# One pass for both norms between the blocks, all taps of three tiles on VectorE, and a layer norm that goes last tile first

## What is computed

```
x = x + gate * attention_output                     # end of block 1
x = rmsnorm(x, final_norm_g)                        # norm A
h = rmsnorm(x, norm_mix_g_2[0])                     # norm B, of the result of norm A
p = h @ w_in_ab_2                                   # a: 512 columns, v: 512, gate: 512
ya = fnet(a)                                        # two DFTs, then a 128x128 map per head
u = v * sigmoid(gate)                               # 4 tiles of 128 channels x 256 tokens
u = depthwise_conv(u, 31 taps) + conv_b
u = layernorm(u over the 128 channels of its tile)  # then silu
x = x + concat(ya, silu(u)) @ w_out_ab_2            # then the first FFN
```

## Time and profile before

| | us |
|---|---|
| median of 3 runs (753.13 to 753.42) | 753.21 |
| the profiled execution, its own time | 753.22 |
| its span, first to last instruction | 751.3 |
| PE busy in it | 724.5 (96%) |
| DVE busy | 509.6 (68%) |
| ACT busy | 396.2 (53%) |

### The profile page before, as it was taken

How to read it: one execution, slowest core, us unless ns; L and a number is a source line. 1 busy time by engine, 2 the same in 40 slices (tenths; PEclk the granted TensorE clock), 3 DMA queues, 4 the chain that set the end, 5 groups by cost and what they waited for, 6 DMA issues and landing times.

```text
span 751.3 us, 9715 instructions
## 1 busy us (share of the span) xinstructions
PE 724.5 (96%) x3898; PEld 626.4 (83%) x3898; DVE 509.6 (68%) x794; ACT 396.2 (53%) x622; POOL 2.4 (0%) x8
## 2 busy tenths in 40 slices
PE   2999999999899999999999999999999999999996
PEld 2888889999899999878888888888788888888885
DVE  5889997998876989986744545454576544545444
ACT  4157446864875677755644344433665344344423
POOL 0000000000000000000000000000000000000000
PEclk9999999999999999999999999999999999999999
DMA  8999983899643525213755445544226455455201
GB/s 339 425 427 413 425 361 147 305 388 348 273 134 149 205 91 210 84 36 161 280 174 203 182 171 198 191 167 172 109 112 224 168 183 205 172 173 198 77 0 57
DMA packets 23229, 156.65 MB, mean 208 GB/s; under 512 B 2576, under 2 KB 2832, under 8 KB 5264
## 3 DMA queue, kind: packets, MB, share of 16 engines
q1 hardware_dynamic: 22608, 153.41, 54.1%
q0 software_dynamic: 576, 2.62, 1.0%
HBM read 154.97 MB, written 1.05 MB: 208 GB/s over the span
## 4 chain that ended last, share of the span: by engine, by line
PE 80%; DVE 10%; ACT 6%; issue 2%; DMA 2%; SPq 0%; DVEq 0%; ACTq 0%
PE pb L1562 20%; PE pb L1563 19%; PE pb L1564 19%; PE pb L1636 13%; DVE w L1009 4%; PE pb L1832 2%; ACT w L611 2%; PE pb L1933 1%; DVE raw L1012 1%; DMA raw<-w_dram 1%; DMA x<-x_dram 1%; DVE t L1009 1%; DVE x L1012 1%; PE pb L1863 1%; PE pb L1875 0%
## 5 line engine op out<-in xcount | busy, mean ns | idle before, releaser
L1009 DVE TENSOR_TENSOR w<-raw,w 128x2048 fp32r<-128x2048 f32 x97 | 221.2, 2290 | 143.6 <-ACT w L611 143.6
L611 ACT ACTIVATE w<-raw 128x2048 fp32r<-128x2048 f32 x97 | 184.8, 1912 | 143.3 <-PE pb L1564 119.2
L1562 PE MATMUL pb<-w,r 128*128 128x512 f32 (+1 forms) x640 | 246.5, 385 | 0.7 <-DVE r L1012 0.4
L1563 PE MATMUL pb<-w,r 128*128 128x512 f32 (+1 forms) x640 | 243.3, 380 | 0.0
L1564 PE MATMUL pb<-w,r 128*128 128x512 f32 (+1 forms) x640 | 243.2, 380 | 0.0
L1562 PEld LDWEIGHTS pb<-w,r 128*128 128x128 f32 x640 | 120.5, 188 | 25.6 <-issue 1.8
L1564 PEld LDWEIGHTS pb<-w,r 128*128 128x128 f32 x640 | 120.5, 188 | 24.7
L1563 PEld LDWEIGHTS pb<-w,r 128*128 128x128 f32 x640 | 120.6, 188 | 23.3
L1562 PE MATMUL pb<-r,w 128*128 128x256 f32 (+1 forms) x352 | 100.3, 285 | 1.0 <-DVE r L1009 0.5
L1563 PE MATMUL pb<-r,w 128*128 128x256 f32 (+1 forms) x352 | 99.4, 282 | 0.0
L1564 PE MATMUL pb<-r,w 128*128 128x256 f32 (+1 forms) x352 | 99.0, 281 | 0.0
(11 more groups left out here) (191 smaller groups left out, 582.6 us busy)
## 6 DMA issues: line engine op xcount, KB each, us to landing
raw<-w_dram SPq DMA_DIRECT2D x129, 1024.0 KB, 4.9
ow<-w_dram SPq DMA_DIRECT2D x8, 1024.0 KB, 15.2
ow<-w_dram SPq DMA_DIRECT2D x8, 512.0 KB, 16.7
oh<-w_dram SPq DMA_DIRECT2D x2, 1024.0 KB, 22.6
x<-x_dram SPq DMA_DIRECT2D x2, 512.0 KB, 5.7
f<-rc_dram POOLq DMA_DIRECT2D x1, 1024.0 KB, 5.0
acc<-row_dram POOLq DMA_DIRECT2D x2, 512.0 KB, 5.2
out_dram<-f SPq DMA_DIRECT2D x4, 256.0 KB, 2.3
```

The costliest lines, as they stand in the source:

```text
L611: return e.activation(out, in_, ACT.Copy, **kw)
L1009: return e.tensor_tensor(out, a, b, op)
L1562: e.matmul(out, a_hi, b_hi, start=start, stop=False)
L1563: e.matmul(out, a_hi, b_lo, start=False, stop=False)
```

## The change

1. Both norms from one pass. `two_squares` makes X² and (g X)² on ACT, `two_adds` sums both on DVE during `project`; PE sums them over channels with four one-column matmuls (`two_sums`), so norm A and norm B are both columns of 128x2. ACT and DVE take roots and reciprocals on those columns, and PE spreads the two results to rows with four 128x128 matmuls (`two_rows`). The second round of squares and adds, and the two reciprocals of 128x256, are gone. Slabs 22 and 23 are done one after the other (`single`), not as a pair.
2. DVE does all 31 taps of tile 2; PE's 12 diagonal taps of it and their addition are gone.
3. The layer norm takes the variance as columns (two one-column matmuls a tile), root and reciprocal on 128x2, and PE spreads the result (`ln_row`, two 128x128 matmuls a tile). The order is tile 3 first, alone, then 0, 1, 2 in groups. `mixed` takes kt 7 before kt 4, and ends with kt 5 and 6.
4. The key projection keeps its raw hi half in a buffer of its own (`KR`) with the shift column beside it; the lo half of the shift is a second column of it. `R2` has no spare columns left. ACT, not DVE, copies the first half of the output into X.

```diff
-NPE = 12
-LN = (0, 1, 3, 2)
+LN = (3, 0, 1, 2)
...
+            def two_squares(d):
+                for m in range(2):
+                    n = 2 * (d - 1) + m
+                    if n >= NT:
+                        p.wait_ge(s_na, 7 + n - NT + 1)
+                    to = tt[n % NT] if d else NA[m]
+                    kw = {"scale": V("final_norm_g", d)} if m else {}
+                    e.activation(to[:, :], X[:, d, :], ACT.Square, **kw).then_inc(s_sq, 1)
...
-                copy(kb[:, d:d + 1], bank_of("k", d)[:, T:T + 1]).then_inc(s_kb, 1)
+                copy(k2[:, :], bank_of("k", d)[:, T:T + 2], accum_out=kb[:, d:d + 1]).then_inc(s_kb, 1)
...
-            row_close(2)
-            col_close(0, rcol[:, 0:2])
+            p.wait_ge(s_rtc, 1)
+            e.reciprocal(rcol[:, 0:2], rcol[:, 0:2]).then_inc(s_rcl, 1)
+            p.wait_ge(s_rcl, 1)
+            tt_(rcol[:, 2:4], sums[:, 2:4], rcol[:, 0:2], MUL).then_inc(s_col, 1)
+            p.wait_ge(s_col, 1)
+            tt_(rcol[:, 2:4], rcol[:, 2:4], rcol[:, 0:2], MUL).then_inc(s_col, 1)
...
+            p.wait_ge(s_rtc, 2)
+            e.reciprocal(rcol[:, 2:4], rcol[:, 2:4]).then_inc(s_rcl, 1)
+            p.wait_ge(s_rcl, 2)
+            tt_(rcol[:, 4:6], rcol[:, 0:2], rcol[:, 2:4], MUL).then_inc(s_col, 1)
             fill(20)
-            p.wait_ge(s_rs, 3)
+            p.wait_ge(s_rsb, 1)
...
             for d in range(2):
                 gated(d, F1[:, 6 + d, :], F1[:, 4 + d, :], (s_b, d + 1), (s_b, d + 3))
+            fill(21)
             for d in range(2, 4):
                 gated(d, out_of("b", 2 + d), out_of("b", 4 + d), ended("b", 2 + d), ended("b", 4 + d))
             fill(22)
...
-            head(20, run("b", 0, 1, 2, 3), 0, lambda: close(2, 0))
-            head(22, run("b", 4, 5, 6, 7), 0, lambda: close(3, 1))
+            first = run("b", 0, 1, 2, 3)
+            pair(20, first, R2, s_rlo, 0, range(6), last=False)
+            two_sums()
+            pair(20, first, R2, s_rlo, 0, range(6, 8), first=False)
+            two_rows()
+            single(22, run("b", 4, 5), R2, s_rlo, 0)
+            single(23, run("b", 6, 7), R2, s_rlo, 0)
...
             def ln_var(d):
                 p.wait_ge(s_lnq, LN.index(d) + 1)
-                e.matmul(PB[OUT.bank["ln", d]][:, 256:512], ones, tt[d][:, :], start=True,
-                         stop=True).then_inc(s_lnv, 1)
+                for a in range(2):
+                    done = e.matmul(bank_of("ln", d)[:, T + a:T + a + 1], tt[d][:, a * P:a * P + P], ones_sb[:, 0:1],
+                                    start=True, stop=True)
+                done.then_inc(s_lnv, 1)
+
+            def ln_row(d):
+                p.wait_ge(s_lni, LN.index(d) + 1)
+                for a in range(2):
+                    done = spread(bank_of("ln", d)[:, T + a * P:T + a * P + P], lnr[:, d, a:a + 1])
+                done.then_inc(s_lnb, 1)
...
+            both(0)
             ln_var(3)
+            both(1)
+            ln_row(3)
+            both(2)
+            ln_mean(0, (s_tap, tap_at[0, 30]))
+            ln_mean(1, (s_tap, tap_at[1, 30]))
             mixed(3, 0, 0, 1)
+            ln_mean(2, (s_tap, tap_at[2, 30]))
             mixed(3, 1, 0, 1)
+            for d in range(3):
+                ln_var(d)
+            mixed(7, 0, 0, 1)
+            for d in range(3):
+                ln_row(d)
+            mixed(7, 1, 0, 1)
+            both(4)
             for a in range(2):
                 for c in range(2):
                     if a and c:
                         turn(0, 0)
-                    for kt in range(4, 8):
+                    for kt in (5, 6):
                         mixed(kt, c, a)
```

More of the change, by code:

```diff
@@ L359, in two_block_program @@
         root = sb("root", [P, T])
-        RS = [sb(f"rs{i}", [P, T]) for i in range(2)]
+        RSt = sb("rs", [P, 2, T])
+        RS = [RSt[:, i, :] for i in range(2)]
         NA = [sb(f"na{i}", [P, T]) for i in range(2)]
@@ L709, in _ @@
             p.wait_ge(s_mv, 11)
[L710 to L712 removed]
+            copy(raw_shift[:, :, 0], mv[:, 4, :]).then_inc(s_shh, 1)
             for d in range(8):
                 p.wait_ge(s_x1, d + 1)
[L715 to L716 removed]
+                e.activation(raw_key(d)[:, 0:T], X[:, d, :], ACT.Copy, scale=mv[:, 3, d:d + 1]).then_inc(s_khi, 1)
+                square(d)
             stream(MATS[2])
@@ L1198, in _, with project @@
                     y_tile(d)
-            def project(kind, i, done, scale, before, raw_, streams):
+            def project(kind, done, scale, before, raw_, add_, streams):
                 for d in range(8):
@@ L1403, in _ @@
             fill(22)
-            pump(12)
-            for c in range(2):
-                fill(24 + c)
-                pump(10)
-            for h in range(4):
-                pump(3)
-            pump(62 - tap_n["n"])
+            pump(36)
+            fill(24)
+            pump(20)
             for h in range(4):
@@ L1787, in _, with two_sums, two_rows @@
             block_of("ao", 16, R1, s_olo, paired=True)
-            def head(k, names, base, then):
-                pair(k, names, R2, s_rlo, base, range(4), last=False)
-                then()
-                pair(k, names, R2, s_rlo, base, range(4, 8), first=False)
-            def close(i, c):
-                row_sum(i)
-                col_sums(c, i)
-            head(20, run("b", 0, 1, 2, 3), 0, lambda: close(2, 0))
-            head(22, run("b", 4, 5, 6, 7), 0, lambda: close(3, 1))
+            def two_sums():
+                bank_free("ns", 0)
+                p.wait_ge(s_na, 7 + 14)
+                for m in range(2):
+                    for a in range(2):
+                        done = e.matmul(bank_of("ns", 0)[:, 2 * m + a:2 * m + a + 1], NA[m][:, a * P:a * P + P],
+                                        ones_sb[:, 0:1], start=True, stop=True)
+                done.then_inc(s_ps, 1)
+            def two_rows():
+                bank_free("rb", 0)
+                p.wait_ge(s_col, 3)
+                for i, c in ((0, 0), (1, 4)):
+                    for a in range(2):
+                        o = i * T + a * P
+                        done = spread(bank_of("rb", 0)[:, o:o + P], rcol[:, c + a:c + a + 1])
+                done.then_inc(s_ps, 1)
+            first = run("b", 0, 1, 2, 3)
[5 more added lines that the diff above has]
+            single(23, run("b", 6, 7), R2, s_rlo, 0)
             for c in range(2):
@@ L1891, in mixed, with both @@
                     done.then_inc(s_half, 1)
-            ln_mean(2, (s_cv2, 1))
-            mixed(0, 0, 0, 1)
-            mixed(0, 1, 0, 1)
-            mixed(1, 0, 0, 1)
+            def both(kt):
+                for c in range(2):
+                    mixed(kt, c, 0, 1)
+            both(0)
             ln_var(3)
-            ln_var(2)
-            mixed(1, 1, 0, 1)
-            mixed(2, 0, 0, 1)
-            mixed(2, 1, 0, 1)
+            both(1)
[3 more added lines that the diff above has]
+            ln_mean(1, (s_tap, tap_at[1, 30]))
             mixed(3, 0, 0, 1)
+            ln_mean(2, (s_tap, tap_at[2, 30]))
             mixed(3, 1, 0, 1)
+            for d in range(3):
+                ln_var(d)
+            mixed(7, 0, 0, 1)
+            for d in range(3):
+                ln_row(d)
+            mixed(7, 1, 0, 1)
+            both(4)
             for a in range(2):
```

339 lines of the change are left out of this document (160 added, 179 removed).

## The result

The changed kernel takes 741.1 us in the median of 4 runs (740.83 to 742.27), the kernel before 753.32 beside it (753.13 to 753.83): ratio 0.984, 95% interval 0.9823 to 0.9857. That is 12.2 us, not 4.8, and outside the predicted range.

What follows compares the result with a forecast made beforehand. The prediction took PE to bound the seam; its terms summed to -5.14 us, +0.3 charged for tight places made -4.8, so 753.22 - 4.8 = 748.4 us, range 747.0 to 750.8.

Steps and rivals of the forecast that it cites:

- Behind 347.3 PE goes on as before, 4.8 earlier: In the two FFNs behind the seam: PE's work keeps its durations and only starts 4.8 us earlier.
- the key part: Key projection: narrower products and one more accumulator read per key, both counted as nothing; 8 unhidden reads some 0.1 each.
- Taps: Convolution on PE: twelve fewer diagonal taps at 0.432 us each, -5.18 us.
- Layer norm on PE and the wait of `ln_var`: Layer norm: PE's sums and rows cost 1.84 us more; the wait for ACT's square goes, -1.15 us.
- Norms: Norms A and B on PE: 1.76 us before, 1.78 after, so +0.02 us.
- Slab 25: PE's wait for slab 25 near 278.78 goes, as DVE has it ready 1.6 us early: -0.67 us.
- The three tight places: `ln_mean(2)`, kt 4, the FFN's first product: +0.3 us charged; rival that they are late, 749.4 to 751.4, chance 0.20.
- three waits of the size that was named: Around tile 3's layer norm: DVE waits for PE three times, 0.5 to 1.5 us each.
- the rival on the other side: DVE becomes the bound: 82 taps at 0.526 us each make PE wait at `ln_mean`, 755.9 us; chance 0.04.
- second pair of table loads: ACT's sqrt and silu loads in the layer norm: hidden; rival, a change costs twice as much, 749.8 us, chance 0.03.
- Cheap one-column products: Norms and layer norm on PE: rival that one-column matmuls in a row cost half of 0.225, 747.0 us; chance 0.05.

Runs made afterwards that it cites:

- old_places: The changed kernel with R2's two unused spare columns back, so R1 and all tensors behind it lie 128 bytes further on: 748.39 us.
- small_aligned: The changed kernel with a 160-byte gap ahead of the constants, putting the small tensors a multiple of 256 bytes from W: 741.10 us.
- plus_16_sums: The changed kernel with the four one-column sums of both norms made five times over, 16 more sums: 746.25 us.

## Why the prediction was wrong

**The step that failed** is "Behind 347.3 PE goes on as before, 4.8 earlier". It took for granted that unchanged code has unchanged durations, and sized the key part by its instructions alone ("both taken as nothing"). No term, no bound and no rival covered that tensors move. What the runs showed in its place: 7.3 us in the FFNs, since R1 came to a whole multiple of 256 bytes from W (5.7) and R2's rows to 1024 bytes (1.6). With the old places the same code takes 748.39, and the forecast was 748.4. That the two agree to a hundredth is luck: the five executions of this run lie 1.4 apart, and errors of 0.1 to 0.25 in the terms below cancel in part.

**The terms of the sum**, from start to start, seam only:

- Taps: predicted -5.18. 13.83 + 4.75 = 18.58 before (the second piece is 312.03 to 316.78), 13.38 after (298.47 to 311.85): -5.20. Right.
- Layer norm on PE and the wait of `ln_var`: predicted +1.84 and -1.15, together +0.69. The sums and rows of the layer norm take 4.22 before with the wait in it, and 4.66 after: +0.44. The wait is gone. The prices were a little high on both sides: six one-column sums take 329.19 to 330.44, 1.25, so 0.21 and not 0.225; a row of 128 columns 0.21 and not 0.22.
- Norms: predicted +0.02; 1.59 before, 1.61 after. Right.
- Slab 25: predicted -0.67. The 288 products of 256 columns in stages b and a take 35.02 before, with the wait in it, 34.38 in old_places and 34.71 after. So the wait gave 0.64, as predicted, and the new places took 0.33 back (0.1200 a product and not 0.1188).
- The three tight places: charged +0.3. PE waits at none, but it was close: DVE's last tap of tile 2 ends at 327.22, and PE begins `ln_mean(2)` at 327.30. What does cost is that the 96 products of the output projection are cut into shorter runs by the sums between them: 22.77 before and 23.19 in old_places, +0.42. The new places give 0.22 of it back (22.97 after). A run of six takes 0.25 to 0.26 each, one of 36 0.23.
- The copies of X through the identity, on which the prediction had no term: -0.08.

In all -5.20 + 0.44 + 0.02 - 0.31 + 0.20 - 0.08 = -4.93, against the -4.8. In the seam the new places take 0.33 from the products of 256 columns and give 0.22 to those of 512. That is why it is about as long with the old places as with the new, and why the places show in the FFNs, whose groups are of 512 columns alone.

**DVE and the rivals.** Timeline of DVE in the changed kernel, against the earlier trace rows:

```profile
278.51 13.15 DVE L1020 SCALAR_TENSOR_TENSOR f<-f,vec 128x256 f32<-128x256 f32 x33
291.58 4.49 DVE L1017 TENSOR_TENSOR w<-raw,w 128x2048 fp32r<-128x2048 f32 x2
...
314.27 0.42 DVE L1020 SCALAR_TENSOR_TENSOR f<-pb,f 128x256 f32<-128x256 f32 x1 [0.83 <-PE pb L1858]
...
322.49 0.48 DVE L1020 SCALAR_TENSOR_TENSOR f<-f,vec,pb 128x256 f32<-128x256 f32 x1 [0.89 <-PE pb L1638]
322.89 2.04 DVE L1020 SCALAR_TENSOR_TENSOR f<-f,vec 128x256 f32<-128x256 f32 x4
324.84 0.42 DVE L1017 TENSOR_TENSOR r<-t,r 128x256 fp32r<-128x256 f32 x1
```

The first 33 taps take 13.07, 0.396 each, as in the kernel before; the four of one tile 1.95, 0.49 each. That is what the prediction's sum has, 1.97 for four, though it names 0.526 each, which would be 2.10. DVE waits at `ln_centre(3)` and `ln_scale(3)` for PE, 0.83 and 0.89, and 1.21 at `ln_inverse(3)` for ACT's root, which itself waits for PE's sum: three waits of the size that was named. So DVE isn't the bound, and the rival on the other side is out. Timeline of ACT at the second pair of table loads, against the earlier trace rows:

```profile
328.90 1.28 ACT L901 ACT_TABLE_LOAD   x1
330.20 0.68 ACT L901 ACTIVATE lnr<-pb,vec 128x2 f32<-128x2 f32 x3
330.90 1.28 ACT L907 ACT_TABLE_LOAD   x1
333.08 0.51 ACT L907 ACTIVATE t<-f,vec 128x256 f32<-128x256 f32 x1 [0.90 <-DVE f L1020]
```

The root starts 1.30 after the load's start, so no drain shows behind it. Silu isn't held by its load, which is done at 332.18, but waits 0.90 more for DVE: the loads are hidden. Cheap one-column products: 0.20 to 0.21, about 0.10 a record as expected from the earlier trace rows and nowhere near a half of 0.225, so out. The first matmuls of the key projection start at 116.1 in this profile and at 114.8 in that of before. In the other profiles they start anywhere from 114.6 to 116.2 with the changed code, and at 115.3 and 115.6 with that of before, so this is no effect that can be put down to the change.

## What to carry to other kernels

When an edit changes a tensor's shape or adds one, print where the tensors behind it come to lie, and treat the products that read them as touched. Where the pace of an untouched stretch changes at the same busy time and the same clock, count instructions in equal windows, then put the old addresses back with a gap: that run tells code from place in one step. Here the products of 512 columns, with W moving, are faster where the distance between their two operands is a multiple of 256 bytes, rows included, and those of 256 columns, with W stationary, are slower there. So look at both kinds before you move a tensor that both read.

## What the runs showed of the hardware

- **The pace of a product depends on the distance between its two operands in SBUF.** For 512 columns it is 0.2267 us at multiples of 256 bytes, 0.2325 at 128 beside one and 0.2335 at 64, over the 48 products with R1 of each group. The Trainium skill, SBUF — State Buffer, section Who interferes with whom, states that PE's two read ports are independent and that "PE and ACT never wait on anyone". By that one would expect the place of the stationary operand to be of no matter to the products; this case's traces disagree by 2.5% of each, and the measurement decides. For 256 columns, with the roles of W and R exchanged, it is 0.1187 at 128 beside, 0.1178 at 64 and 0.1200 at a multiple. Whether the two reads meet in the memory, and why the sign turns (the number of columns or the roles), is not shown.
- **The pace has to settle.** In the changed kernel's run of 36 products of the output projection (333.18 to 341.50) the first 13 or so start 0.23 or 0.24 apart, and only the rest in the steady 0.23, 0.23, 0.22. With the old places the same run never settles: 8.48 in place of 8.32. A run of 6 or 12 between sums has little to gain. In the FFNs the 24 products with R2 come first behind a turn, which may be a part of why R2 is worth less than R1. Why it settles stays open.
- **Float32 products and turns don't show it:** small_aligned is equal to the changed kernel within its spread, and the diagonal taps take 0.432 us each in both.
- **TensorE's clock can fall while its records show no idle time.** Before it fell to 1.2 GHz in plus_16_sums, PE had done nothing but one-column sums since 258.43. The transfers that run beside them (DMA share 0.94 to 0.97 from 260 to 262) run in the changed kernel too (1.05 from 262 to 263), at a clock of 1.00. The Trainium skill, TensorE: Matmul & The Clock Gate, section What's actually happening, says that the gate follows how busy PE has been; the busy column here says 1.00 throughout, and the clock fell all the same.
